# The first modulation of a two-block transformer kernel: TensorE takes over the last two of its eight summed pieces

## What is computed

```
c_act = jax.nn.silu(c)
for layer in range(DEPTH):
    mod = c_act @ ada_w[layer] + ada_b[layer]
    sh_m, sc_m, gt_m, sh_f, sc_f, gt_f = [m[:, None, :] for m in jnp.split(mod, 6, axis=-1)]
    h = modulate(rms_norm(x, norm_mix_g[layer]), sh_m, sc_m)
    mix = hybrid_mixer(h, w_in[layer], ...)
    x = x + gt_m * mix
    ...
```

## Time and profile before

| | |
|---|---|
| median of three runs | 2190.22 us (2187.6 to 2191.72) |
| profiled execution | 2186.8 us, of which its span 2184.9 us |
| TensorE (PE) busy in the span | 2137.1 us, 98% |
| VectorE (DVE) busy | 1736.2 us, 79% |
| ScalarE (ACT) busy | 1238.5 us, 57% |
| mean granted clock of TensorE | 0.989 |

### The profile page before, as it was taken

One profiled execution on the slowest core, in us unless ns is written; L12 is line 12 of the kernel. 1 busy time (PEld: TensorE's weight loads), 2 busy tenths in 40 slices (PEclk: granted clock), 3 DMA queues, 4 the chain that ended last, 5 costly groups with the idle time before them and its releaser, 6 DMA issues.

```text
span 2184.9 us, 33385 instructions
## 1 busy us (share of the span) xinstructions
PE 2137.1 (98%) x13865; PEld 1921.1 (88%) x13865; DVE 1736.2 (79%) x1875; ACT 1238.5 (57%) x1398; POOL 54.2 (2%) x101
## 2 busy tenths in 40 slices
PE   6999999999999999999999999999999999999999
PEld 5989999987888788878888889888999998889998
DVE  5998777878899899989898977777766677756666
ACT  2734444736677677777777764552455445524554
POOL 1010000000000000000000000000000000000000
PEclk8999999999999999999999999999999999999999
DMA  9887985747999999999999986737555466345552
GB/s 312 311 302 281 334 313 184 254 160 274 363 381 365 365 370 376 351 374 374 370 363 382 379 281 178 254 132 252 210 174 187 122 177 213 116 135 174 174 183 88
DMA packets 339039, 578.55 MB, mean 265 GB/s; under 512 B 48098, under 2 KB 208954, under 8 KB 326594
## 3 DMA queue, kind: packets, MB, share of 16 engines
q1 hardware_dynamic: 324604, 475.34, 63.7%
q0 software_dynamic: 13824, 100.67, 11.9%
q10 hardware_dynamic: 454, 0.34, 0.1%
HBM read 575.26 MB, written 1.05 MB: 264 GB/s over the span
## 4 chain that ended last, share of the span: by engine, by line
PE 82%; DVE 9%; DMA 4%; ACT 3%; issue 2%; DVEq 0%; ACTq 0%; POOL 0%; SPq 0%; POOLq 0%
PE bank L598 81%; DVE w_low L2149 3%; DMA ring<-in_moe_w 2%; DMA ada_in<-in_ada_w 2%; DVE ada_acc L2157 1%; ACT arena L1583 1%; DVE arena L2157 1%; PE bank L1341 1%; DVE arena L2149 1%; DMA ring<-in_ffn_w 1%; DVE arena L2634 1%; ACT mix_hi L1583 0%; ACT L1583 0%; DVE arena L2434 0%; DVE h_low L2157 0%
## 5 line engine op out<-in xcount | busy, mean ns | idle before, releaser
L1583 ACT ACTIVATE moe_w_hi<-ring 128x2048 fp32r<-128x2048 f32 x264 | 506.4, 1919 | 177.4 <-DMA ring<-in_moe_w 139.5
L2149 DVE TENSOR_TENSOR w_low<-ring,moe_w_hi 128x2048 fp32r<-128x2048 f32 x264 | 594.5, 2285 | 15.6 <-ACT moe_w_hi L1583 11.5
L598 PE MATMUL bank<-h_hi,w_hi 128*128 128x256 f32 x1056 | 258.4, 284 | 1.1 <-ACT h_hi L1583 0.9
L598 PE MATMUL bank<-h_hi,w_low 128*128 128x256 f32 x1056 | 257.9, 281 | 0.0
L598 PE MATMUL bank<-mix_h_hi,w_low 128*128 128x256 f32 (+2 forms) x848 | 239.0, 284 | 0.0
L598 PE MATMUL bank<-mix_h_hi,mix_hi 128*128 128x256 f32 x800 | 231.3, 292 | 3.9 <-DVE w_low L2149 2.2
L598 PE MATMUL bank<-h_low,mix_hi 128*128 128x256 f32 x800 | 213.8, 283 | 0.0
L2157 DVE SCALAR_TENSOR_TENSOR ada_acc<-ada_in,c_col,ada_acc 128x2048 f32<-128x2048 f32 x84 | 197.3, 2348 | 16.7 <-DMA ada_in<-in_ada_w 11.7
L598 PEld LDWEIGHTS bank<-h_hi,w_hi 128*128 128x128 f32 x1056 | 198.8, 188 | 2.6 <-issue 2.1
L598 PEld LDWEIGHTS bank<-h_hi,w_low 128*128 128x128 f32 x1056 | 200.2, 190 | 0.1
L2149 DVE TENSOR_TENSOR w_low<-ring,w_hi 128x2048 fp32r<-128x2048 f32 (+1 forms) x67 | 150.3, 2273 | 52.0 <-ACT w_hi L1583 51.2
(11 more groups left out here) (224 smaller groups left out, 4542.6 us busy)
## 6 DMA issues: line engine op xcount, KB each, us to landing
ring<-in_moe_w SPq DMA_DIRECT2D x264, 1024.0 KB, 6.8
ada_in<-in_ada_w POOLq DMA_DIRECT2D x96, 1024.0 KB, 7.6
ring<-in_w_in SPq DMA_DIRECT2D x56, 1024.0 KB, 5.5
ring<-in_ffn_w_up SPq DMA_DIRECT2D x44, 1024.0 KB, 7.7
ring<-in_ffn_w SPq DMA_DIRECT2D x33, 1024.0 KB, 8.3
ring<-in_ffn_w_down SPq DMA_DIRECT2D x22, 1024.0 KB, 4.9
ring<-in_w_out SPq DMA_DIRECT2D x16, 1024.0 KB, 5.4
ring<-in_w_br_mla SPq DMA_DIRECT2D x4, 1024.0 KB, 5.7
```

The source lines that it names most:

```text
L598: ins = nc.tensor.matmul(out, lhsT, rhs, start=start, stop=stop, skip_group_check=shared)
L1583: return nc.scalar.activation(out, in_, f, **kw)
L2149: return nc.vector.tensor_tensor(out, a, b, op)
```

## The change

VectorE multiplies and adds six pieces instead of eight, and TensorE sums `ada_acc` over the partitions after the sixth. The last two pieces go to TensorE as they are loaded: a block of the piece is the weights, and the column of `c_act`, repeated 32 times, moves; the results add up in PSUM on top of the first sums. The sums are 32 columns wide (before 64). The eight sums of the scale stand in bank 0 and come first, the eight of the shift in bank 7. VectorE makes the scale and two blocks of `h` as soon as bank 0 is whole, and adds the shift's bias after that. `keep_busy(12)` becomes `keep_busy(3)`. The load of the unit rgx 0 waits for three used pieces instead of five, and the next load on SyncE's queue, rgx 1, for six, where it had no wait of its own; the small tables stand behind it.

```diff
--- before.py
+++ after.py
@@ -43,6 +43,8 @@
+FIRST_WIDE = 32
+FIRST_ADDED = KB - 2
...
@@ -490,7 +492,9 @@
                 if key == ("rgx", 0, 0):
-                    sp.wait_ge(s["ada_used"], KB - ADA_SLOTS)
+                    sp.wait_ge(s["ada_used"], ADA_SLOTS)
+                if key == ("rgx", 0, 1):
+                    sp.wait_ge(s["ada_used"], FIRST_ADDED)
...
@@ -741,6 +745,28 @@
+            def first_modulation():
+
+                halves = ((0, KB), (7, 0))
+                need("ada_done")
+                for b, j0 in halves:
+                    fill(b)
+                    for j in range(KB):
+                        mm(bank[b][:, j * FIRST_WIDE:(j + 1) * FIRST_WIDE],
+                           ada_acc[:, 0, (j0 + j) * P:(j0 + j + 1) * P], ones[:, 0:FIRST_WIDE],
+                           start=(j == 0), stop=False, shared=True)
+                need("c_act")
+                for kb in range(FIRST_ADDED, KB):
+                    slot, last = ada_slot[kb], kb == KB - 1
+                    scalars = c_col[:, 0, kb:kb + 1].to_broadcast([P, FIRST_WIDE])
+                    pe.wait_ge(ada_full[slot], 16 * ada_count[kb])
+                    for b, j0 in halves:
+                        for j in range(KB):
+                            done = j == KB - 1 and ("mod_psum" if last else "ada_used" if j0 == 0 else None)
+                            mm(bank[b][:, j * FIRST_WIDE:(j + 1) * FIRST_WIDE],
+                               ada_in[:, slot, (j0 + j) * P:(j0 + j + 1) * P], scalars,
+                               start=False, stop=last, shared=True, inc=done or None)
...
@@ -785,7 +811,7 @@
-                keep_busy(12)
+                keep_busy(3)
...
@@ -1504,7 +1530,7 @@
             start()
-            start_modulation()
+            first_modulation()
             mixer1(0)
...
@@ -2277,17 +2303,32 @@
                 need("c_act")
-                for n in range(KB):
+                for n in range(FIRST_ADDED):
                     ada_piece(n)
-                    if n == KB - 3:
-                        need("norm_std")
-                        nc.vector.reciprocal(region(2048, T), region(2304, T))
-                dve.wait_ge(s["ada_used"], KB)
+                dve.wait_ge(s["ada_used"], FIRST_ADDED)
                 dve.sem_inc(s["ada_done"], 1)
+                need("norm_std")
+                nc.vector.reciprocal(region(2048, T), region(2304, T))
                 need("vcol_ready")
                 low(("rgx", 0, 0))
-                modulation(0, 0, 2 * KB, 0)
-                scaled(scale_a[:, 0, :], h, "norm_mul")
+
+                def sums(b):
+                    return bank[b][:, 0:KB * FIRST_WIDE].rearrange("p (j c) -> p j c", j=KB)[:, :, 0]
+
+                need("mod_psum")
+                tell(tt(mod[:, KB:2 * KB], sums(0), vcol[:, 0, KB:2 * KB], ALU.add), None, 0)
+                settle(stt(scale_a[:, 0, :], mod[:, KB:2 * KB], 1.0,
+                           vcol[:, 0, PACK1["norm_mix"]:PACK1["norm_mix"] + KB], ALU.add, ALU.mult))
+                ahead = 2
+                for kb in range(ahead):
+                    stt(h[:, kb, :], x[:, kb, :], scale_a[:, 0, kb:kb + 1], region(2048, T), ALU.mult, ALU.mult)
+                need("mod_psum")
+                dve.sem_inc(s["ada_used"], 1)
+                tell(tt(mod[:, 0:KB], sums(7), vcol[:, 0, 0:KB], ALU.add), None, 7)
+                dve.sem_inc(s["norm_mul"], ahead)
+                for kb in range(ahead, KB):
+                    stt(h[:, kb, :], x[:, kb, :], scale_a[:, 0, kb:kb + 1], region(2048, T), ALU.mult, ALU.mult)\
+                        .then_inc(s["norm_mul"], 1)
```

## The result

The changed kernel took 2194.51 us (median of 20 runs, 2187.2 to 2200.14), the kernel before 2187.39 (20 runs, 2181.52 to 2193.28): 7.1 us slower by the medians. The ratio is given as 1.0029, 95% interval 1.0018 to 1.0040, which is 6.3 us. Comparisons here leave disturbed runs out. The profiled execution took 2193.75 us, its span 2191.9, where the kernel before had 2184.9. The time lies inside the range of the prediction, but the forecast shift was +1.2 and the measured one is +7.1; the change is slower by more than 0.2%, to which the prediction had given 0.18.

The account below looks back on a forecast made before the run. TensorE, busy 98% of the span, was taken as the bound. Narrow matmuls ending at 47.2, plus 0.2 drain and 1.1 tail, put the mixer at 48.5 against 47.30; 2190.22 + 1.2 = 2191.4 us, range 2184 to 2196.5.

Parts of the forecast that it names:

- the likeliest case: The clock falls in the middle of the 96 narrow matmuls: 2189.8 to 2192.3 us, chance 0.62.
- the 4.3 taken and the bounds 3.3 and 6.1: Microseconds until the clock falls, read from earlier rows: 4.3 after 32-column matmuls began, with 3.3 and 6.1 as bounds.
- The tail: From the last modulation matmul to the mixer's first: 1.1 us instead of 1.73, as the scale is made earlier.
- Costing the unit loads at nothing: Moving the rgx 0 and rgx 1 loads adds no time, being covered by 7 us and more; uncovered, 2 us.
- the base of the forecast: Median of three runs of the kernel before, 2190.22 us, to which the shift of 1.2 was added.
- The clock holds: Rival: full clock through all 96 narrow matmuls, 6.0 us sooner together, 2184.2 us; chance 0.14.
- Narrower is cheaper: Rival: matmul cost goes by columns, 0.055 us at full clock; mixer 5.9 to 7.6 us sooner, about 2183.5; chance 0.03.
- The clock never rises: Rival: with three constants instead of twelve, the modulation stays at half clock; 6.1 us later, 2196.3 us; chance 0.13.
- The loads collide: Rival: rgx 0, asked for earlier, goes ahead of piece 6; 1.5 us more, 2192.9 us; chance 0.08.
- When they can start: The first group of narrow matmuls starts at 30.77, when the six remaining constant instructions end.
- Rows done before the fall: With the fall at 35.1, 39 of 96 narrow instructions are done; 57 remain at 0.213 us, 12.1 us.
- The rise behind the mixer's start: The clock rises after the mixer starts as before, 2.9 us, with half of 0.5 us as uncertainty.

Follow-up runs that it names:

- e2: The changed kernel with the loads of rgx 0 and rgx 1 back at the waits of before; 2193.68 us, ratio 1.0027 to the kernel before.
- e6: The changed kernel with twelve constant matmuls instead of three; 2196.93 us (six runs), ratio 1.0048 to the kernel before.
- e5: The kernel before with only the two unit loads moved; 2187.47 us, ratio 0.9997 to the kernel before.
- e1: The changed kernel with its 48 matmuls 64 columns wide instead of 32; 2188.36 us, ratio 0.9997 to the kernel before.
- e3: The kernel before with three constant matmuls instead of twelve; 2188.65 us, ratio 1.0008 to the kernel before.
- e7: The changed kernel with all eight pieces on VectorE again, the rest kept; 2188.6 us, ratio 1.0007 to the kernel before.
- e10: e8 with the two unit loads moved; 2184.4 us, ratio 0.9994 to the kernel before.
- e4: The changed kernel with seven pieces on VectorE, one on TensorE, 64 columns, ten constant matmuls; 2188.57 us, ratio 1.0008 to the kernel before.
- e11: e8 run again, unchanged; 2185.78 us, ratio 0.9998 to the kernel before.
- e8: The changed kernel with all eight pieces on VectorE, 64 columns, sixteen constant matmuls, old loads; 2183.14 us, ratio 0.9988 to the kernel before.
- e9: The changed kernel 64 columns wide and with the old unit loads; 2189.98 us, ratio 1.0020 to the kernel before.

## Why the prediction was right, and where its size was off

**Right.** The path ran as laid out: the six constants, then 96 narrow instructions without idle time, first at the full clock, then at half, with the data never deciding (no wait for piece 6 or 7). The clock fell in the middle of the narrow work, the likeliest case: 4.1 us after it began in the changed kernel, 5.8 in e2, 3.9 in e6, against the 4.3 taken and the bounds 3.3 and 6.1. The instructions cost 0.111 us at 1.00, as many columns or few, and 0.213 at 0.50, also at 32 columns, which no row of before could show. The tail was 1.15 us (1.1 forecast). Costing the unit loads at nothing held in the time (e2, e5), though one sign failed: ScalarE was to have rgx 0 before 36.

```profile
37.11 2.00 ACT L1609 ACTIVATE mix_hi<-ring 128x1024 fp32r<-128x1024 f32 x2 [7.65 <-DMA ring<-in_w_in]
```

Asked for 9.2 us sooner (18.61 against 27.78), it came only 1.4 us sooner than in the earlier trace rows. Its parts were still done by 40.63, long before the mixer.

**Luck.** Beyond the mechanism, the hit owes something to the base of the forecast. The three runs that it started from have a median 2.8 us above that of twenty. As a shift, the likeliest case was -0.4 to +2.1 us and the upper end of the range +6.3; the measured 6.3 (ratio) to 7.1 (medians) lies at that end or beyond it, nearer to the rival that never rises (+6.1) than to the forecast. And the 4.3 us was read off a place where 64-column matmuls stood on both sides of the 32-column ones, which had ended 0.6 us before the clock fell at 1303.0; it was not quite the same work. The row of the kernel before behind the last of the earlier trace rows:

```profile
1302.21 2.96 PE L598 MATMUL bank<-const,ada_acc 128*128 128x64 f32 x16
```

**The rivals.** *The clock holds* did not happen at 32 columns; it is what happens at 64 (e1: mixer at 44.35). The Trainium skill, "TensorE: Matmul & The Clock Gate", section "HAM oscillation — how this bites in real kernels", asks only that TensorE avoid long idle gaps; here it had none (13.32 of 13.40 us busy, at 0.50), as in e6, and lost the clock. *Narrower is cheaper* fell: 0.111 us at both widths, each instruction with a weight load of its own. *The clock never rises* came near: its condition was a rise that takes more than about 5 us, and it took 6.0 (26.78 to 32.8). The full clock did come, but 0.7 us into the narrow work, and left 3.4 us later. *The loads collide* fell as named: TensorE never waits for a piece.

**The terms that were mis-sized.** The forecast +1.2 was +3.37 at the mixer's first matmul and +4.67 behind its first projection. In the order of the sum:

- *When they can start.* 30.77 forecast, 32.09 measured. The parameters landed 0.4 us later (26.78; the other profiles have 25.63 to 27.21), and the six constants, under which the clock had risen before, ran at 0.50 to their end (4.11 us). With the 4.1 us that the clock held from there, the fall lies at 36.2 instead of 35.1: 1.1 of the difference.
- *Rows done before the fall.* 39 forecast, 35 measured (96 less the 61 that follow: the 63 rows of that stretch take in the cut ones), as the first 0.7 us ran at half the pace: 4 x 0.213, 0.9 more. These two make 2.0 of the 2.2 us between 48.5 and 50.67.
- *The rise behind the mixer's start.* Taken as 2.9 with half of 0.5 us as the uncertainty; measured 6.0 us (50.67 to 56.7). Three more microseconds with the mixer's instructions 0.213 us apart instead of 0.12 are the 1.3 between +3.37 and +4.67. This was the worst judged of the terms: in the profiles in which the mixer started at the low clock the rise took 2.9 (before), 6.0 (after), 3.1 (e2), 5.4 (e3), 3.3 (e5), 2.9 (e6), 3.8 (e7) and 3.1 (e10). Two rows of one trace, 3.4 and 2.9, were taken for its whole spread.

**What lies beyond the beginning.** 7.1 us in the medians (6.3 by the ratio) against 4.7 in one pair of profiles leaves 1.6 to 2.4. The prediction held that a shift of the mixer's first matmul reaches the end nearly unchanged. In single executions it did not: +3.37 ended at +7.0 in the changed kernel, -2.95 at +2.8 in e1, -2.6 at -5.2 in e4. Each run lists its mean granted clock: 0.9845 on average over the 20 runs of the changed kernel, 0.9879, 0.9873 and 0.9887 over the runs of before in the three groups. At the first of these, 0.0034 x 2190 is 7.4 us of lost clock, about the whole difference (6.1 and 9.2 at the others; the twenty runs of before beside the changed kernel have no clock on record); over the 20 runs time and clock correlate at -0.89. e1 has 0.9879, as before, and is as fast as before; e3 and e7 have 0.9852 and 0.9855 and are hardly slower, but they idle 8 us in this stretch, partly at the low clock, where that costs nothing. All that agrees with the loss being clock, the narrow stretch above all; but no trace shows how the beginning went in the 19 other runs, and whether the usual one lost 7 there or 4.7 there and the rest at later falls is open. The FFN's wait of 1.6 us near 205 also stands in the profiles of e1, e4, e6 and e7 (1.5 to 2.0), all with the moved loads, and not in those with the old loads (0.4 at most). e5 has the moved loads, costs nothing and has 0.4 us of the wait, e10 has them and 0.5 us; the cause is not settled. A second wait of 1.08 us at 258.7 stands in e5, e7 and e11 too (about 1.0) and not in e1, e4 and e6.

**Where e1's gain went.** It has the mixer 2.95 us sooner and 2.08 of that left at 150 us; its profile then shows the long fall (0.50 from 158.8 to 172.5) and is 3.2 behind at 182, 5.3 behind the wait. e4 is 2.3 ahead at 142 and 0.4 behind at 202, yet 5.2 ahead at the end: its profiled execution was the fastest of its twelve. Over all runs nothing of the 2 us is to be seen. That the start at another moment makes the later falls longer was not shown: e8 and e10 have the mixer at about the same time and the short fall, e11 the long one.

## What to carry to other kernels

Before work goes from VectorE to TensorE as many small matmuls, read the granted clock of the stretch and not only the busy share: here 32-column fp32 matmuls in an unbroken row lost the clock and 64-column ones at the same cost per instruction kept it. The width alone was worth 6.3 us at its place and 7 in the time (e1), but with the old loads 1.5 us, which the runs do not tell from nothing (e9 against e2). A forecast that rests on when a clock rises or falls should take its spread from all places of the trace at which it does so, and from more than one execution. A gain of 2 us at one place of a 2190 us kernel whose runs scatter by 12 has to be shown in more runs than the twelve that each version had here, whose intervals reach some 3 us to either side; the row of the profile is not enough.

## What the runs showed of the hardware that was not expected

- Width against clock at the same spacing: an fp32 matmul instruction with its own 128 x 128 weights comes every 0.111 us with 32 or 64 columns moving. Three kernels with 32 columns at the full clock lost it 3.9 to 5.8 us in (after, e2, e6); six with 64 (e1, e4, e8 to e11) kept it through 3.7 to 10.7 us of such work. All six lost it for 3.4 us soon after: 0.3 to 1.8 us behind the mixer's start, in e10 0.4 us ahead of it. The kernel before and e5, where 2.2 to 2.5 us without work stood ahead of the 64-column matmuls, lost it 0.8 and 1.0 us into them.
- The rise took between 3.1 us (e5, 26.27 to 29.33) and 6.0 us (after) behind the start of the same eight transposes and the constants, and between 2.9 and 6.0 behind the mixer's start.
- The fall near 159 us (157.2 to 168.0) lasted 3.4 us in eight of the profiles and 13.7 to 17.1 us in four (e1, e3, e5, e11); the profiled execution of the changed kernel had none there. e8 and e11 are the same kernel and fall on either side. The length went with the place of the fall beside the wait of 2.19 us that all thirteen profiles have there: short when it came between 0.5 us before the wait's end and 0.8 us after it, long at 1.1 before (e5) and at 1.3 to 1.5 after (e1, e3, e11). No run tested that.
- A unit asked for 9.2 us earlier on SyncE's queue came 1.4 us earlier and did not hold back pieces 6 and 7 where TensorE could notice. Piece 5 reached VectorE at 29.06 against 27.93; in the other kernels with the moved loads it came at 27.77 to 28.97, so no more than a part of that 1.1 us is the load.
